# Recurrent scan of an HGRN layer: the levels in another order, three of them read by one copy, the diagonal as two products

## The reference

```python
def hgrn2_scan(q, k, v, logf, s0):          # chunks of Q tokens
    def step(S, inp):
        qc, kc, vc, gc = inp
        bcs = jnp.cumsum(gc, axis=1)
        o_inter = jnp.einsum('bthk,bhkv->bthv', qc * jnp.exp(bcs), S)
        diff = bcs[:, :, None] - bcs[:, None]
        dec = jnp.exp(jnp.where(mask[None, :, :, None, None], diff, -jnp.inf))
        att = jnp.einsum('bthk,btshk,bshk->bhts', qc, dec, kc)
        o_intra = jnp.einsum('bhts,bshv->bthv', att, vc)
        ...
```

## Time and profile before

| | us |
|---|---|
| median of 3 runs | 2948.34 (2928.3 to 2952.78) |
| the profiled execution | 2944.84 |
| its span | 2943.1 |
| granted TensorE clock, mean | 0.918 of 2.4 GHz |
| the scan of the 8 heads | about 1724 to 1918 us of the span |

### The profile page before, as it was taken

One profiled execution on the slowest core, in us unless ns is written; L12 is line 12 of the kernel. 1 busy time (PEld: TensorE's weight loads), 2 busy tenths in 40 slices (PEclk: granted clock), 3 DMA queues, 4 the chain that ended last, 5 costly groups with the idle time before them and its releaser, 6 DMA issues.

```text
span 2943.1 us, 30331 instructions
## 1 busy us (share of the span) xinstructions
PE 2631.5 (89%) x11898; PEld 1938.1 (66%) x11898; DVE 1455.2 (49%) x2125; ACT 747.8 (25%) x1260; POOL 800.2 (27%) x445
## 2 busy tenths in 40 slices
PE   5688999998898889899998877689999899989997
PEld 3688864446887778744458866676444699974444
DVE  7446543335547776633336388874333506650013
ACT  1132221003353342301014344432000234230111
POOL 3355400002443254000014468830000247500000
PEclk8889989998799999899998888988999899979999
DMA  7533649891330215388943411043889243428881
GB/s 272 172 115 114 215 153 336 323 348 56 104 115 30 72 58 172 124 331 318 360 167 136 138 52 35 20 157 137 337 322 347 71 144 101 143 101 295 299 296 44
DMA packets 291854, 524.43 MB, mean 178 GB/s; under 512 B 9472, under 2 KB 141056, under 8 KB 291328
## 3 DMA queue, kind: packets, MB, share of 16 engines
q1 hardware_dynamic: 288256, 519.33, 50.2%
q10 hardware_dynamic: 3456, 3.15, 0.3%
HBM read 517.73 MB, written 4.72 MB: 178 GB/s over the span
## 4 chain that ended last, share of the span: by engine, by line
PE 75%; DVE 12%; ACT 4%; issue 3%; DMA 3%; POOL 2%; SPq 0%; ACTq 0%; DVEq 0%
PE ps L1839 23%; PE ps L1854 11%; PE ps L1589 6%; PE ps L1590 6%; PE ps L1591 6%; PE ps L1654 3%; DVE macc L1926 2%; POOL wlo L1521 2%; PE ps L1612 1%; PE ps L1778 1%; PE ps L1613 1%; PE ps L1614 1%; PE ps L1802 1%; PE ps L1803 1%; PE ps L1682 1%
## 5 line engine op out<-in xcount | busy, mean ns | idle before, releaser
L1521 POOL TENSOR_TENSOR wlo<-ring,whi 128x1024 fp32r<-128x1024 f32 x202 | 526.0, 2620 | 1500.2 <-ACT whi L1388 1500.1
L1839 PE MATMUL ps<-ring,xg 128*128 128x512 f32 x1536 | 707.3, 605 | 0.0
L1839 PEld LDWEIGHTS ps<-ring,xg 128*128 128x128 f32 x1536 | 290.1, 194 | 329.3 <-issue 328.9
L1926 DVE SCALAR_TENSOR_TENSOR macc<-ring,cond_s,macc 128x1024 f32<-128x1024 f32 x322 | 436.4, 1416 | 10.0 <-DMA ring<-w_mod 10.0
L2144 DVE SCALAR_TENSOR_TENSOR hid<-ps,cws,sg 128x256 f32<-128x256 f32 x96 | 46.5, 484 | 673.0 <-ACT sg L1482 673.0
L1854 PE MATMUL ps<-ring,hidt 128*128 128x512 f32 x768 | 350.2, 599 | 2.3 <-ACT hidt L1457 2.3
L1589 PE MATMUL ps<-hh,whi 128*128 128x384 f32 x832 | 305.1, 367 | 25.4 <-POOL wlo L1521 19.1
L1591 PE MATMUL ps<-hh,wlo 128*128 128x384 f32 x832 | 291.8, 351 | 0.0
L1590 PE MATMUL ps<-hl,whi 128*128 128x384 f32 x832 | 291.7, 351 | 0.0
L1388 ACT ACTIVATE whi<-ring 128x1024 fp32r<-128x1024 f32 x202 | 206.9, 1053 | 299.7 <-DMA ring<-gmlp_w_out 111.5
L1854 PEld LDWEIGHTS ps<-ring,hidt 128*128 128x128 f32 x768 | 147.5, 193 | 187.6 <-issue 187.6
(11 more groups left out here) (347 smaller groups left out, 4217.4 us busy)
## 6 DMA issues: line engine op xcount, KB each, us to landing
ring<-moe_w_gu SPq DMA_DIRECT2D x192, 1024.0 KB, 7.6
ring<-w_mod SPq DMA_DIRECT2D x96, 1024.0 KB, 7.9
ring<-moe_w_down SPq DMA_DIRECT2D x96, 1024.0 KB, 5.0
ring<-gmlp_w_in SPq DMA_DIRECT2D x32, 1024.0 KB, 5.8
ring<-ssd_w_in SPq DMA_DIRECT2D x21, 1024.0 KB, 5.3
ring<-hgrn_w_in SPq DMA_DIRECT2D x20, 1024.0 KB, 5.3
ring<-gmlp_w_out SPq DMA_DIRECT2D x16, 1024.0 KB, 5.8
ring<-ssd_w_out SPq DMA_DIRECT2D x8, 1024.0 KB, 5.8
```

Of the source, the lines that this page charges most:

```text
L1521: pool.tensor_tensor(split_sub(wlo, s0), raw_sub(s0), split_sub(whi, s0).bitcast(F32), ALU.subtract).then_inc(S["lo_ready"], 1)
L1839: ins = pe.matmul(ps[:, s % 2, :], xg[:, w, k, :], whole(what, s, 4)[:, k % 4, :], start=(k == 0), stop=(k == KD - 1))
L1926: ins = dve.scalar_tensor_tensor(out=macc[:, v, :], in0=w[:, k, :], scalar=by, in1=macc[:, v, :], op0=ALU.mult, op1=ALU.add)
```

## The change

The levels go from wide to narrow: step j is now level 6 - j for j = 0 to 6, and step 7 is the diagonal. The three widest levels (`JOINT` = 3) are written into the same bank. Level 6 (step 0) fills it with three products of 128 columns; level 5 (step 1) overwrites the six diagonal blocks of 64 x 64; level 4 (step 2) overwrites the twelve of 32 x 32. Then one plain copy reads the bank into `att`; there is no pick in steps 0 and 1. Levels 3 to 0 are picked as before. The diagonal no longer uses a buffer: PE adds two products, each of one direction's key with q, and the pick takes it by a predicated copy with the identity as mask. The buffers are numbered by level alone, so `produce` and `complete` run two and one levels ahead. `carry` moves from steps 1 and 2 to 2 and 3, with a wait for the previous head's output. `pick_of` counts the picks that lie before a step, `step_of` gives the step of a level.

```diff
@@ -981,7 +981,7 @@
                     n = LEVELS * h + j
                     act.wait_ge(S["u_sub"], n + 1)
                     act.wait_ge(S["w_sub"], n + 1)
-                    uw = uw_slot(HL * h + j + 1)
+                    uw = uw_slot(n)
                     act.activation(uw[:, :, :], uw[:, :, :], ACT.Exp).then_inc(S["u_exp"], 1)
                     if j == 0:
                         if h:
@@ -1050,8 +1050,19 @@
         HL = LEVELS + 1
         NS = HH * HL
-        def uw_slot(n):
-            return uws[n % 3]
+        JOINT = 3
+        def uw_slot(m):
+            return uws[m % 3]
+        def step_of(m):
+            return HL * (m // LEVELS) + m % LEVELS
+        def pick_of(g):
+            return (HL - JOINT + 1) * (g // HL) + max(0, g % HL - JOINT + 1)
         def pool_hgrn(pool, l, feed):
             pool.memset(hmask[:, :], 1.0).then_inc(S["hmask_set"], 1)
@@ -1062,11 +1073,10 @@
             pool.wait_ge(S["q_evac"], 8)
             def decay(n):
-                h, j = divmod(n, LEVELS)
-                g = HL * h + j + 1
-                if g >= 3:
-                    pool.wait_ge(S["lv_done"], g - 2)
-                out = uw_slot(g)[:, 1, :].rearrange("p (b two x) -> p b two x", two=2, x=1 << j)
+                h, j = n // LEVELS, LEVELS - 1 - n % LEVELS
+                if n >= 3:
+                    pool.wait_ge(S["lv_done"], step_of(n - 3) + 1)
+                out = uw_slot(n)[:, 1, :].rearrange("p (b two x) -> p b two x", two=2, x=1 << j)
                 pool.tensor_tensor(out, crossed(h, j), border(h, j, True), ALU.subtract).then_inc(S["w_sub"], 1)
             decay(0)
@@ -1075,7 +1085,7 @@
                 if n + 1 < LEVELS * HH:
                     decay(n + 1)
                 pool.wait_ge(S["u_exp"], n + 1)
-                W = uw_slot(HL * h + j + 1)[:, 1, :]
+                W = uw_slot(n)[:, 1, :]
                 pool.tensor_tensor(W, W, hq[:, h, :], ALU.mult).then_inc(S["wq_ready"], 1)
                 if j == 4:
                     pool.wait_ge(S["qe_exp"], h + 1)
@@ -1155,7 +1165,7 @@
                           stop=True).then_inc(S["hst_done"], 1)
             def output(h):
-                pe.wait_ge(S["lv_read"], HL * (h + 1))
+                pe.wait_ge(S["lv_read"], pick_of(HL * (h + 1)))
                 pe.wait_ge(S["qe_ready"], h + 1)
                 pe.wait_ge(S["hs1_ready"], 2 * h + 2)
                 if h:
@@ -1176,14 +1186,21 @@
             state(0, 3)
             for n in range(NS):
                 h, j = divmod(n, HL)
-                pe.wait_ge(S["uw_ready"], n + 1)
-                if j:
-                    pe.wait_ge(S["wq_ready"], LEVELS * h + j)
-                if n >= 2:
-                    pe.wait_ge(S["lv_read"], n - 1)
-                for t in range(NT):
-                    rhs = uw_slot(n)[:, 1, toks(t)] if j else hq[:, h, toks(t)]
-                    ins = pe.matmul(ps[:, n % 2, toks(t)], uw_slot(n)[:, 0, toks(t)], rhs, start=True, stop=True)
+                if j < LEVELS:
+                    pe.wait_ge(S["uw_ready"], LEVELS * h + j + 1)
+                    pe.wait_ge(S["wq_ready"], LEVELS * h + j + 1)
+                    U, W = uw_slot(LEVELS * h + j)[:, 0, :], uw_slot(LEVELS * h + j)[:, 1, :]
+                if pick_of(n) >= 2 and not 0 < j < JOINT:
+                    pe.wait_ge(S["lv_read"], pick_of(n) - 1)
+                width = P >> j if j < JOINT else P
+                for c in range(0, T, width):
+                    t, r = divmod(c, P)
+                    o, cut = ps[r:r + width, pick_of(n) % 2, c:c + width], slice(c, c + width)
+                    if j < LEVELS:
+                        ins = pe.matmul(o, U[:, cut], W[:, cut], start=True, stop=True)
+                    else:
+                        pe.matmul(o, hk[:, 0, h, cut], hq[:, h, cut], start=True, stop=False)
+                        ins = pe.matmul(o, hk[:, 1, h, cut], hq[:, h, cut], start=False, stop=True)
                 ins.then_inc(S["lv_done"], 1)
                 if j == 0 and h:
                     state(h, 3)
@@ -1200,7 +1217,7 @@
                         state(h + 1, 2)
             output(HH - 1)
             square_sums(HH - 1)
-            for b, v in ((0, ("lv_read", 64)), (1, ("lv_read", 64)), (2, ("hstd", 1)), (3, ("hg_act", HH)),
+            for b, v in ((0, ("lv_read", pick_of(NS))), (1, ("lv_read", pick_of(NS))), (2, ("hstd", 1)), (3, ("hg_act", HH)),
                          (4, ("khT_read", 32)), (5, ("khT_read", 32)), (6, ("hs1_ready", 16)), (7, ("hs1_ready", 16))):
                 release[b] = (S[v[0]], v[1])
             pe.wait_ge(S["rr_ready"], 1)
@@ -1269,54 +1286,55 @@
             def produce(g):
-                h, j = divmod(g, HL)
-                if j:
-                    if g >= 3:
-                        dve.wait_ge(S["lv_done"], g - 2)
-                    out = uw_slot(g)[:, 0, :].rearrange("p (b two x) -> p b two x", two=2, x=1 << (j - 1))
-                    dve.tensor_tensor(out, border(h, j - 1), paired(hf_flat, h, j - 1), ALU.subtract).then_inc(S["u_sub"], 1)
+                h, j = g // LEVELS, LEVELS - 1 - g % LEVELS
+                if g >= 3:
+                    dve.wait_ge(S["lv_done"], step_of(g - 3) + 1)
+                out = uw_slot(g)[:, 0, :].rearrange("p (b two x) -> p b two x", two=2, x=1 << j)
+                dve.tensor_tensor(out, border(h, j), paired(hf_flat, h, j), ALU.subtract).then_inc(S["u_sub"], 1)
             def complete(g):
-                h, j = divmod(g, HL)
-                out = uw_slot(g)[:, 0, :]
-                if j:
-                    dve.wait_ge(S["u_exp"], LEVELS * h + j)
-                    out = out.rearrange("p (b two x) -> p b two x", two=2, x=1 << (j - 1))
-                    dve.tensor_tensor(out, out, paired(hk_flat, h, j - 1), ALU.mult).then_inc(S["uw_ready"], 1)
-                else:
-                    if g >= 3:
-                        dve.wait_ge(S["lv_done"], g - 2)
-                    dve.tensor_tensor(out, hk[:, 0, h, :], hk[:, 1, h, :], ALU.add).then_inc(S["uw_ready"], 1)
+                h, j = g // LEVELS, LEVELS - 1 - g % LEVELS
+                out = uw_slot(g)[:, 0, :].rearrange("p (b two x) -> p b two x", two=2, x=1 << j)
+                dve.wait_ge(S["u_exp"], g + 1)
+                dve.tensor_tensor(out, out, paired(hk_flat, h, j), ALU.mult).then_inc(S["uw_ready"], 1)
             a3 = att[:, :].rearrange("p (t n) -> p t n", t=NT)
             def pick(g):
                 h, j = divmod(g, HL)
+                if j < JOINT - 1:
+                    return
                 dve.wait_ge(S["lv_done"], g + 1)
-                dve.wait_ge(S["lv_read"], g)
-                src = bank(g % 2).rearrange("p (t n) -> p t n", t=NT)
-                if j == 0:
+                dve.wait_ge(S["lv_read"], pick_of(g))
+                src = bank(pick_of(g) % 2).rearrange("p (t n) -> p t n", t=NT)
+                if j == JOINT - 1:
                     if h:
                         dve.wait_ge(S["o_done"], h)
-                    ins = dve.tensor_tensor(a3, src, ident[:, :].unsqueeze(1).to_broadcast([P, NT, P]), ALU.mult)
+                    ins = dve.tensor_copy(a3, src)
                 else:
-                    ins = dve.copy_predicated(a3, lvl[:, j - 1, :].unsqueeze(1).to_broadcast([P, NT, P]), src)
+                    mask = lvl[:, LEVELS - 1 - j, :] if j < LEVELS else ident[:, :].bitcast(U32)
+                    ins = dve.copy_predicated(a3, mask.unsqueeze(1).to_broadcast([P, NT, P]), src)
                 ins.then_inc(S["lv_read"], 1)
             for i in range(4):
                 key(0, i)
                 key_turned(0, i)
+            produce(0)
             produce(1)
             complete(0)
             for g in range(NS):
                 h, j = divmod(g, HL)
-                if g + 2 < NS:
-                    produce(g + 2)
-                if g + 1 < NS:
-                    complete(g + 1)
-                if j in (1, 2):
-                    carry(h, j + 1)
+                m = LEVELS * h + j
+                if j < LEVELS:
+                    if m + 2 < LEVELS * HH:
+                        produce(m + 2)
+                    if m + 1 < LEVELS * HH:
+                        complete(m + 1)
+                if j in (2, 3):
+                    if h:
+                        dve.wait_ge(S["o_done"], h)
+                    carry(h, j)
                 if h + 1 < HH:
                     if 3 <= j <= 6:
                         key_turned(h + 1, j - 3)
```

## The result

The changed kernel takes 2979.58 us (median of 4 runs, 2972.83 to 2984.49) against 2941.81 of the kernel before measured with it: ratio 1.0125 [1.0099, 1.0151]. It is slower by 38 us of the medians; the profiled spans are 2974.8 and 2943.1 us, 31.7 apart. Of the ten executions of experiment 5's kernel, one (4168.81 us, at a granted clock of 0.58) is left out of its ratio.

What follows compares the result with a forecast made beforehand. DVE and POOL taking turns bound the scan; a closed chain of 4.6 us less 1.4 gained gives +3.2 a head, 22.4 over seven, less 0.75 and 1.5: +20 us. Forecast 2967 us, range 2939 to 2992.

Steps and rivals of the forecast that it cites:

- the first rival: Scan's chain runs at TensorE's lower clock: +2 us a head, +34 (30 to 42) in all, 2982 us; chance 0.19.
- The bound: In the scan, POOL operations and DVE products on SBUF operands take turns, covering 22.5 of 23.8 us a head.
- The gains: Per scan head, 0.41 us of turns saved plus at most 1.3 of free time closed: 0.4 to 1.7, taken 1.4.
- the second rival: DVE and POOL run a step ahead in the scan, hiding the chain: gain of 3 to 14 us, 2940; chance 0.24.
- The chain, step 2 to step 3: Scan time from step 2's TensorE product to step 3's, through transpose, key decay and exponent 3: 5.9 us, before 2.83.
- The narrow records: Step 2's 24 TensorE records of 32 columns: 0.95 us taken, 0.66 to 3.2 as bounds, +0.25 over a wide step.
- The chain, step 3 to step 4: Scan time from step 3's product to step 4's, exponent 4 behind key decay 3: 4.3 us, before 2.80.
- The state copies: ACT's state copies delay later exponents, but DVE's keys and picks and a POOL product, about 5 us, hide it.
- The sum: Net per scan head with key work: chain 4.6 us less gains 1.4, +3.2 us; seven such heads 22.4 us.
- The rival on the other side: The second rival: cover in the scan makes the change faster, if step 2 to step 3 stays under 3 us.
- The third: Rival: narrow TensorE records in steps 1 and 2 each cost a full matmul, +6 us a head, 3016 us; chance 0.05.
- a cost for changing the width of the products: Changing tiling mode drains TensorE in the scan: some 1 us a head more, +28 in place of +20 us.

Runs made afterwards that it cites:

- experiment 5: Changed kernel with only the next head's key transposes (and DVE's keys and copies) one step earlier, state products left in steps 4 and 5: 2939.17 us, 0.9978.
- experiment 7: Experiment 1 with POOL's weight operation held for DVE's last product, plus: POOL product cut 2931.77 us; two more picks 2942.32; output copies later 2944.77; gate products first 2935.51.
- experiment 1: Changed kernel with the next head's key work (transposes, state products, key products and copies) one step earlier: 2933.24 us, 0.9964 of the kernel before.
- experiment 4: Changed kernel with 12, 6 and 3 useless 64-column products added on TensorE in steps 2, 3 and 4 to keep it warm: 2969.19 us, 1.0081.

## Why the prediction was right, point by point

The direction and the mechanism were right: a chain through TensorE, ACT and DVE closes, and costs more than the change gives. The size was too small, and that the time still came near the forecast is in part luck.

- **The time.** 2967 us forecast, 2979.6 measured. But the forecast counted from a median before of 2948.3, and measured together with the change that median is 2941.8. The loss was forecast at +20 us and is 38 between the medians, 32 between the profiled spans, 30 in the scan. That is the first rival's loss (30 to 42), which had a chance of 0.19 against 0.52. For a loss over 29.5 us the prediction had 0.20 in all.
- **The bound.** Taking turns between POOL and DVE's products fits experiment 7: 0.95 us less cover is 0.95 us less head, and 1.16 us of picks are none in a middle head.
- **The gains.** "0.4 to 1.7; I take 1.4" us a head. Experiment 1 has them without the chain: 23.83 - 22.11 = 1.7 us, the upper end. They come in another split than was said. The cover fell from 22.5 to 21.6, by 0.9 us and not 0.41, and the free time from 1.3 to 0.5. For the kernel the second rival had 3 to 14 us; experiment 1 gained 12.
- **The chain, step 2 to step 3.** 5.9 us forecast, 5.27 measured. The narrow records were over-priced: 0.40 us for 24, where the prediction took 0.95 and bounded them from below by 0.66. That bound rested on halving the pace of the nearest row, and the row says nothing of how far such records overlap.
- **The chain, step 3 to step 4.** 4.3 us forecast, 5.57 measured. From product to ACT's waking it is 2.89 us (1826.98 to 1829.87), not 1.68, since TensorE is at half clock there. At full clock the term was right: experiment 4 has 4.3 us. This is the term that was mis-sized. The first rival had it, at +2 us a head; experiment 4 gives back 1.8 us in the head shown and 1.3 in the mean of five.
- **The state copies.** The prediction let DVE's keys and picks hide them. In the changed kernel DVE waits 1.1 us there; experiment 5 shows that this, too, is a consequence of the transposes' place.
- **The sum.** +3.2 us a head forecast, 28.2 - 23.83 = +4.4 measured. The measured terms give about that: 5.27 - 2.83 and 5.57 - 2.80 for the two links, 1.1 for the state copies, less 1.7 of gains, is 4.6. A chain that makes TensorE idle was priced at full clock, and the overpriced narrow records hid a part of the error.
- **The rival on the other side** (cover) is refuted by the waits: nothing runs ahead, and step 2 to step 3 takes 5.27 us where it asked for under 3. The third (dear narrow records) as well, and of a cost for changing the width of the products (some 1 us a head) no idle time shows at 1848.12. The wait of the first pick for the output (1.40 us) has gone, as forecast.
- **Signs named beforehand.** Right: the wait of 2.5 us ahead of DVE's product in step 2 (2.5 to 3.5 named); ACT waiting for the transpose in both places; POOL's longer waits for ACT; the last head, from the seventh head's output to its own, 1.0 us shorter (18.6 and 17.6 us; 1 to 2 named); outside the stage all but 1.5 us of the spans' difference unchanged. Missed: the wait in step 3, 2.9 us where 1 to 2 were named; the head, 28.2 us where 26 to 27.5 were; and POOL's busy time, which went up by 0.8 us a head and not down, since its operations' lengths include their waits for the turn.

## What to carry to other kernels

When a pipeline's steps are renumbered, everything on an engine's queue that was attached to the old numbers must move with them. Here an exponential was asked for one step earlier, while what stood before it on ACT's queue kept its place, and the price was 28.2 - 22.1 = 6 us a head, more than three times the 1.7 us that the change itself gives. Before counting instructions saved, ask which resource they use: in a middle head two picks of 0.58 us were free, and 0.95 us less of what POOL and DVE cover together was worth 0.95 us. And where two engines take turns, which of them starts a long operation first is part of the schedule: write the order down with a wait rather than leave it to 0.4 us of chance.

## What was not expected of the hardware

- 24 matmul records of 32 x 32 take 0.40 us from the first start to the last end, where one of them lasts 0.19 to 0.22: they start about 0.01 us apart. Twelve of 64 columns take 0.57 us.
- A shorter POOL operation made the kernel slower by 13 us (2946.26 against 2933.24), because it let a 2.7 us POOL operation get in ahead of a DVE product. One wait brought 14 us back.
- In the changed kernel the granted clock falls in, or right behind, a TensorE idle time of 4.05 us, and the products behind it run at half clock (1.62 us for six wide records against 0.94). That puts a price on a wait beyond its length: about 15 us of each middle head of 28 ran so.
